# Router logits inside the normalisation, router parameters on SyncE's queue, and one stage for collecting the experts' rows and the final norm

## The reference

```python
def hier_moe(h, w_rg, b_rg, w_re, b_re, w_gate, w_up, w_down):
    ...
    g_logits = hf @ w_rg.astype(jnp.float32) + b_rg.astype(jnp.float32)
    ...
    top_v, top_i = lax.top_k(e_in_group, TOP_K)
    weights = jax.nn.softmax(top_v, axis=-1) * g_w
    ...
    def expert_block(args):
        xi, e = args
        return (jax.nn.silu(xi @ w_gate[e]) * (xi @ w_up[e])) @ w_down[e]
```

## Time and profile before

| | |
|---|---|
| median of three runs | 4025.27 us (4022.03 to 4025.39) |
| the profiled execution | 4030.13 us, its span 4028.2 us |
| TensorE busy | 3414.9 us, 85% of the span |
| VectorE, ScalarE, GpSimd busy | 39%, 27%, 16% |
| mean granted clock of TensorE | 0.922 |
| moved by DMA | 534.00 MB, mean 133 GB/s |

### The profile page before, as it was taken

The page is one execution under the profiler, slowest core; times in us unless marked ns, Lnnn a source line. Parts: engine busy times, 40 slices in busy tenths (PEclk is TensorE's granted clock), DMA queues, the critical chain, the costliest instruction groups (busy, mean ns, idle before and its releaser), DMA issues.

```text
span 4028.2 us, 41123 instructions
## 1 busy us (share of the span) xinstructions
PE 3414.9 (85%) x16083; PEld 2352.7 (58%) x16083; DVE 1570.6 (39%) x2654; ACT 1107.3 (27%) x1925; POOL 647.8 (16%) x471
## 2 busy tenths in 40 slices
PE   4996765787882998788999799999599888988998
PEld 2664543222231884445886488888485456856886
DVE  3226642000004356563333433333474563425444
ACT  3112411112112225443221222221234543303221
POOL 1000001000003325122220100000245223401000
PEclk8998876889996999899999899999799999998999
DMA  6883022799995311002112211111521002233222
GB/s 257 334 314 128 1 105 65 304 427 428 428 429 195 100 44 22 9 1 84 63 63 94 94 63 63 63 63 50 176 81 33 9 35 101 85 110 120 89 93 79
DMA packets 159784, 534.00 MB, mean 133 GB/s; under 512 B 9532, under 2 KB 64724, under 8 KB 136572
## 3 DMA queue, kind: packets, MB, share of 16 engines
q1 hardware_dynamic: 136252, 401.04, 26.9%
q0 software_dynamic: 16880, 92.26, 6.6%
q10 hardware_dynamic: 6480, 38.34, 2.4%
HBM read 488.84 MB, written 42.78 MB: 132 GB/s over the span
## 4 chain that ended last, share of the span: by engine, by line
PE 59%; DVE 4%; ACT 2%; DVEq 1%; DMA 1%; issue 1%; POOL 0%; ACTq 0%; POOLq 0%
PE ps L2774 11%; PE ps L2780 11%; PE ps L1840 7%; PE ps L1842 7%; PE ps L1841 7%; PE ps L511 5%; PE ps L2053 4%; PE ps L2105 2%; PE ps L2093 2%; PE ps L2087 1%; DVE Z L2677 1%; DMA ring<-in_w_out_dram 1%; DVE small L2193 0%; DVE hT_hi L2681 0%; DMA xl<-xspill 0%
## 5 line engine op out<-in xcount | busy, mean ns | idle before, releaser
L2774 PE MATMUL ps<-hT_hi,w_hi 128*128 128x512 f32 (+1 forms) x768 | 275.6, 359 | 27.9 <-DVE w_lo L2828 27.9
L2774 PE MATMUL ps<-hT_hi,w_lo 128*128 128x512 f32 (+1 forms) x768 | 276.4, 360 | 0.0
L2774 PE MATMUL ps<-hT_lo,w_hi 128*128 128x512 f32 (+1 forms) x768 | 275.8, 359 | 0.0
L1840 PE MATMUL ps<-wp_hi,hT_hi 128*128 128x512 f32 (+2 forms) x608 | 222.6, 366 | 37.2 <-POOL wp_lo L1819 37.2
L2780 PE MATMUL ps<-w_hi,h_hi 128*128 128x512 f32 x640 | 253.7, 396 | 0.0
L2780 PE MATMUL ps<-w_hi,h_lo 128*128 128x512 f32 x640 | 253.7, 396 | 0.0
L2780 PE MATMUL ps<-w_lo,h_hi 128*128 128x512 f32 x640 | 253.6, 396 | 0.0
L2053 PE MATMUL ps<-Z 64*128 64x256 f32 (+3 forms) x576 | 202.1, 548 | 28.2 <-DVE small L2195 12.5
L2493 POOL TENSOR_TENSOR mr_lo<-ring,wm_hi 128x2048 fp32r<-128x2048 f32 x36 | 170.7, 4754 | 312.1 <-ACT wm_hi L2485 312.0
L1842 PE MATMUL ps<-wp_hi,hm_lo 128*128 128x512 f32 (+2 forms) x608 | 220.8, 363 | 0.0
L1841 PE MATMUL ps<-wp_lo,hT_hi 128*128 128x512 f32 (+2 forms) x608 | 220.2, 362 | 0.0
(11 more groups left out here) (443 smaller groups left out, 6492.7 us busy)
## 6 DMA issues: line engine op xcount, KB each, us to landing
pj<-in_expert_w_up_dram SPq DMA_DIRECT2D x32, 2048.0 KB, 18.3
pj<-in_expert_w_down_dram SPq DMA_DIRECT2D x32, 2048.0 KB, 19.7
ring<-in_expert_w_gate_dram SPq DMA_DIRECT2D x32, 2048.0 KB, 15.9
ring<-in_ffn_w_dram SPq DMA_DIRECT2D x64, 1024.0 KB, 5.2
ring<-in_w_in_dram SPq DMA_DIRECT2D x58, 1024.0 KB, 5.3
Z<-in_w_mod_dram POOLq DMA_DIRECT2D x24, 2048.0 KB, 8.1
Z<-in_w_ada_dram POOLq DMA_DIRECT2D x8, 2048.0 KB, 9.0
ring<-in_w_out_dram SPq DMA_DIRECT2D x6, 2048.0 KB, 16.2
```

What stands on the lines that cost most here:

```text
L1840: nc.tensor.matmul(out_, a_hi, b_hi, start=first, stop=False)
L2774: last = nc.tensor.matmul(bank(i % 8, c1 - c0), W[a][:, k, :], r[:, k, c0:c1], start=(k == 0 and r is hhk and a == 0), stop=(k == KT - 1 a ...
```

## The change

- The logits of tile t are computed inside the normalisation, as soon as its evacuations are in, behind the transposes of tile t + 1. `pe_norm` calls `each` for this. They go to bank 4. The fence between normalisation and routing is gone.
- The seven parameter loads are issued by SP, one stage earlier, ahead of the context tile and the experts' first weights. Their place in `Z` moves.
- `fng` and the gates are loaded at the start of the experts' stage.
- The collection has buffers for all four tiles, in `pj`, so that the eight gathers are issued without a wait. ScalarE makes the first of the four passes over a tile (scaling by the first weight) and squares each tile when VectorE has added it. Collection and final norm are one stage.

```diff
                     last.then_inc(mm_done, 1)
+                if t:
+                    each(p, t - 1)
+            each(p, nt - 1)
             n["xn"] += nt
...
         XK = lambda t: Z[:, 1024 + 1024 * t:2048 + 1024 * t]
-        rw = Z[:, 5200:5488].rearrange("p (k n) -> p k n", k=KT)
-        rb = Z[:, 5488:5524]
+        rw = Z[:, 10240:10528].rearrange("p (k n) -> p k n", k=KT)
+        rb = Z[:, 10528:10564]
...
-        def pool_route_params(pool):
-            pool.dma_start(rw[:, :, 0:NG], I["router_group_w"][0].rearrange("(k p) n -> p k n", p=P)).then_inc(rparams, 16)
-            pool.dma_start(rw[:, :, NG:NG + NE], I["router_expert_w"][0].rearrange("(k p) n -> p k n", p=P)).then_inc(rparams, 16)
-            pool.dma_start(rb[:, 0:NG], I["router_group_b"][0].partition_broadcast(P)).then_inc(rparams, 16)
-            pool.dma_start(rb[:, NG:NG + NE], I["router_expert_b"][0].partition_broadcast(P)).then_inc(rparams, 16)
+        def sp_route_params(sp):
+            sp.dma_start(rw[:, :, 0:NG], I["router_group_w"][0].rearrange("(k p) n -> p k n", p=P)).then_inc(rparams, 16)
+            sp.dma_start(rw[:, :, NG:NG + NE], I["router_expert_w"][0].rearrange("(k p) n -> p k n", p=P)).then_inc(rparams, 16)
+            sp.dma_start(rb[:, 0:NG], I["router_group_b"][0].partition_broadcast(P)).then_inc(rparams, 16)
+            sp.dma_start(rb[:, NG:NG + NE], I["router_expert_b"][0].partition_broadcast(P)).then_inc(rparams, 16)
             for dst, src in ((fsh, modd[0, 0, 3 * D:4 * D]), (fsc, modd[0, 0, 4 * D:5 * D]), (fga, I["norm_ffn_g"][0])):
-                pool.dma_start(dst, src.rearrange("(p k) -> p k", k=KT)).then_inc(rparams, 16)
+                sp.dma_start(dst, src.rearrange("(p k) -> p k", k=KT)).then_inc(rparams, 16)
+
+        def pool_route_rows(pool):
             pool.memset(ZERO, 0).then_inc(zero_ok, 1)
...
+        def pe_logits(pe):
+
+            def each(p, t):
+                if t == 0:
+                    pe.wait_ge(rparams, 16 * 7)
+                for i in (2 * t, 2 * t + 1):
+                    pe.wait_ge(EV[p.own[i]], p.val[i])
+                for k in range(KT):
+                    last = nc.tensor.matmul(bank(4)[:, 36 * t:36 * t + 36], hTk[:, k, 128 * t:128 * t + 128], rw[:, k, :],
+                                            start=(k == 0), stop=(k == KT - 1))
+                if t == TL - 1:
+                    last.then_inc(mm_done, 1)
+            return each
+
         def pe_route(pe, n):
             p = plan_route(n)
-            pe.wait_ge(rparams, 16 * 7)
-            for t in range(TL):
-                for k in range(KT):
-                    last = nc.tensor.matmul(bank(0)[:, 36 * t:36 * t + 36], hTk[:, k, 128 * t:128 * t + 128], rw[:, k, :],
-                                            start=(k == 0), stop=(k == KT - 1))
-            last.then_inc(mm_done, 1)
             n["v2p"] += 1
...
                 for u in range(t + 1):
-                    last = nc.tensor.matmul(bank(1)[:, 32 * t:32 * t + 32], C(C_US) if u == t else C(C_ONE), oh[:, u, :],
+                    last = nc.tensor.matmul(bank(5)[:, 32 * t:32 * t + 32], C(C_US) if u == t else C(C_ONE), oh[:, u, :],
                                             start=(u == 0), stop=(u == t))
...
             for u in range(TL):
-                last = nc.tensor.matmul(bank(2)[:, 0:32], C(C_ONE), oh[:, u, :], start=(u == 0), stop=(u == TL - 1))
+                last = nc.tensor.matmul(bank(6)[:, 0:32], C(C_ONE), oh[:, u, :], start=(u == 0), stop=(u == TL - 1))
             last.then_inc(mm_done, 1)
...
-        yg = [[Z[:, 1024 * (2 * i + c):1024 * (2 * i + c) + 1024] for c in range(2)] for i in range(2)]
+        yg = [[pj[:, 1024 * (2 * i + c):1024 * (2 * i + c) + 1024] for c in range(2)] for i in range(TL)]
         fng = Z[:, 4608:5632]
...
-        def pool_comb(pool, n):
+        def pool_comb(pool):
             for t in range(TL):
-                if t >= 2:
-                    pool.wait_ge(yg_free, t - 1)
                 for c in range(2):
-                    pool.indirect_dma_start(yg[t % 2][c], None, ybuf, bass.IndirectOffsetOnAxis(ap=IDX[:, c, t:t + 1].bitcast(U32), axis=0)
-                                            ).then_inc(yg_in[t % 2], 16)
+                    pool.indirect_dma_start(yg[t][c], None, ybuf, bass.IndirectOffsetOnAxis(ap=IDX[:, c, t:t + 1].bitcast(U32), axis=0)
+                                            ).then_inc(yg_in[t], 16)
...
             for t in range(TL):
-                dve.wait_ge(yg_in[t % 2], 32 * (t // 2 + 1))
-                y0, y1 = yg[t % 2]
-                nc.vector.tensor_scalar(y0, y0, WT[0][:, t:t + 1], None, ALU.mult)
-                dve.drain()
+                dve.wait_ge(y0_ok, t + 1)
+                y0, y1 = yg[t]
                 nc.vector.scalar_tensor_tensor(y0, y1, WT[1][:, t:t + 1], y0, ALU.mult, ALU.add)
...
         def act_final(act, n):
-            act.wait_ge(yg_free, TL)
-            for t in range(TL):
-                act.activation(junk, xl[:, t, :], ACT.Square, accum_out=st[:, t:t + 1])
-                act.drain()
+            for t in range(TL + 1):
+                if t < TL:
+                    act.wait_ge(yg_in[t], 32)
+                    act.activation(yg[t][0], yg[t][0], ACT.Copy, scale=WT[0][:, t:t + 1]).then_inc(y0_ok, 1)
+                if t:
+                    act.wait_ge(yg_free, t)
+                    act.activation(junk, xl[:, t - 1, :], ACT.Square, accum_out=st[:, t - 1:t])
+                    act.drain()
             act.activation(st[:, 16:20], st[:, 0:4], ACT.Copy).then_inc(sumsq, 1)
...
             sp.wait_ge(stage_done, 4 * 10)
+            sp_route_params(sp)
             sp.dma_start(xl[:, TL:TA, :], I["ctx_2"][0].rearrange("(t p) d -> p t d", p=P)).then_inc(x_in, 16)
...
             plan_route(n)
-            sp.wait_ge(stage_done, 4 * 13)
+            sp.wait_ge(stage_done, 4 * 12)
             sp_moe(sp)
-            n["fence"] = 4 * 16
+            n["fence"] = 4 * 14
             plan_attn(n, *da_spec())
-            sp.wait_ge(stage_done, 4 * 16)
+            sp.wait_ge(stage_done, 4 * 14)
             for l in range(2):
...
                 fence(pool, n)
-            pool_route_params(pool)
-            fence(pool, n)
+            pool_route_rows(pool)
             pool_route(pool)
...
             fence(pool, n)
+            pool.dma_start(fng, I["final_norm_g"].partition_broadcast(P)).then_inc(fng_in, 16)
             pool_moe(pool)
             fence(pool, n)
-            pool.dma_start(fng, I["final_norm_g"].partition_broadcast(P)).then_inc(fng_in, 16)
-            pool_comb(pool, n)
-            fence(pool, n)
+            pool_comb(pool)
             fence(pool, n)
...
             fence(pe, n)
-            pe_norm(pe, n, TL, keep=XK)
-            fence(pe, n)
+            pe_norm(pe, n, TL, keep=XK, each=pe_logits(pe))
             pe_route(pe, n)
...
             pe_moe(pe)
-            fence(pe, n)
             fence(pe, n)
...
             act_norm(act, n, TL, 0, 1)
-            fence(act, n)
             act_route(act, n)
...
             fence(act, n)
+            load_gate(act, 0, 5)
             act_moe(act)
-            fence(act, n)
-            load_gate(act, 0, 5)
             fence(act, n)
...
             dve_norm(dve, n, TL, 0, 1, keep=XK)
-            fence(dve, n)
             dve_route(dve, n)
...
             dve_comb(dve, n)
-            fence(dve, n)
             dve.wait_ge(fng_in, 16)
...
             fence(dve, n)
```

More of the change, by code:

```diff
@@ L213, in program @@
         ex_used, ybz = sem("ex_used"), sem("ybz")
-        yg_in, fng_in = [sem("yg_in0"), sem("yg_in1")], sem("fng_in")
+        yg_in, fng_in, y0_ok = [sem(f"yg_in{i}") for i in range(4)], sem("fng_in"), sem("y0_ok")
         def tally():
```

10 lines of the change are left out of this document (5 added, 5 removed).

## The result

The changed kernel took 4002.87 us (median of 6 runs, 3997.96 to 4010.23), the kernel before 4027.38 beside it (median of 6). The ratio of the changed kernel's time to the time before is 0.9941, 95% interval 0.9926 to 0.9956: faster by 0.6%, some 24 us. The forecast was 3997.3 with a range of 3991 to 4007, so the time lies in the range, and the forecast gain of 28.0 was some 4 us too much.

The account below looks back on a forecast made before the run. Serial stretches before and after the experts' DMA-bound weight stream were taken to bound what can be saved. 17.4 - 1.5 + 12.1 = 28.0 us off the median 4025.27 gives 3997.3, range 3991 to 4007.

Parts of the forecast that it names:

- Logits: Normalisation: logits between transposes, no fence, bring VectorE's bias add 17.4 us earlier, bounds 14.3 and 20.4.
- the middle: Logits' end taken as 657.9, between 661.0 at 1.2 GHz and 654.9 at 2.4 GHz; gain 17.4 us.
- The upper bound: Logits at 2.4 GHz from 644.8, ending at 654.9: gain 20.4 us; part of a rival given 15 in 100.
- Parameters through SyncE: Seven small loads in SyncE's queue ahead of the weights: cost nothing, covered 68 us; weights out some 8 us later.
- The same 22 us of VectorE work follow: Routing behind the logits: VectorE's work unchanged, so GpSimd's first scatter moves along with the bias add.
- part 1: Logits computed within the normalisation, fence removed: gain 17.4 us.
- The moved loads: Start of the experts: fng by GpSimd, gates by ScalarE; cost 1.5 us, from 0 to 3.7.
- Contention: Start of the experts: moved loads share bandwidth with the first gather, at most 2.8 us within the 3.7 bound.
- Collection and final norm: Behind the experts: gathers without buffer waits, ScalarE scaling, one square left at the end; gain 12.1 us, bounds 9.3 and 12.7.
- Part 3: The change to collection and final norm: gain 12.1 us.
- The stream carried its start along: Experts' weight stream keeps its length, 508 to 509 us; second trip's SP loads about 16 us earlier. Opposite rival: 5 in 100.
- gathers as slow as before: Rival at the collection: 8.1 us landing is the gathers' own, gain there 9.3, sum 25.2, 4000.1 us; 17 in 100 for this end.

Follow-up runs that it names:

- e7: e5 plus 512-column filler matmuls on TensorE ahead of the normalisation, behind the logits, behind the rank matmuls and ahead of the experts' loop; 3992.65 us, ratio 0.9904.
- e9: e5 with all four tiles' transposes ahead of all logits, one stage, no fence, no fillers; 3998.67 us, ratio 0.9918.
- e11: e5 plus filler matmuls ahead of the normalisation, behind the logits and behind each of the first three logit groups; 3991.04 us, ratio 0.9905.
- e3: Kernel before with only the logits inside the normalisation and the parameters by SyncE; 4013.75 us, ratio 0.9967.
- e5: Changed kernel with fng and only the gate row that is read loaded by SyncE behind the first expert weights, into pj's unused end; 3995.62 us, ratio 0.9916.
- e10: Changed kernel with the seven parameter loads issued by GpSimd at the start of the normalisation again, without the fence; one run, 4013.83 us.
- e4: Kernel before with only the new collection, gates and fng loaded by ScalarE at the start of the experts; 4020.49 us, ratio 0.9982.
- e2: Changed kernel with the two gates loaded at the start of the collection again, fng still by GpSimd ahead of its loop; one run, 4002.57 us.
- e1: Changed kernel with fng issued by ScalarE behind the gates instead of by GpSimd ahead of its loop; 4004.86 us, ratio 0.9945.

## Why the prediction came out as it did

- **Logits: the mechanism right, the size off within its bounds.** Forecast 17.4 as the middle of 14.3 and 20.4; the profile gave 14.7, which is the end at 1.2 GHz, with its unit price of 3.47 a tile exact (the earlier trace rows against 647.89, 3.47). Among the profiles of programs with this order and no fillers the middle does not occur: they fall at 20.6 or at 13.0 us, to the bias add. The upper bound (20.4) was itself low, for 35.26 - 13.06 is 22.2; at the higher clock 32 records of logits took 3.66 us, 1.83 a tile, and not the 2.18 priced as transposes. Values between exist where the clock changed on the way under another program (e7 17.9, e9 and e11 16.0). Six profiles don't say how often each level comes, so the middle as a mean over executions is not shown either. The rule of the Trainium skill that the prediction weighed (TensorE: Matmul & The Clock Gate, part 1, the HAM clock gate), sustained matmul activity releases the throttle, holds in the profiles of e3 and e5 and not in those of the changed kernel and of before, where 20.5 and 13.87 us of unbroken work stayed at 0.50, nor at the end of e9's logits, where the clock fell during such work.
- **Parameters through SyncE: right at no cost, wrong in the numbers.** Seven loads were expected to take SP 8 us; they took 3.6 (574.66 to 578.22), the weights went out 2.8 us later than before (578.70 against 575.89), and each parameter landed 1.9 to 2.6 us after its issue. The prediction priced the change of queue at nothing beside the logits. e10 shows that it carried 9.7 us of them. It also called the zeroing the dearest per byte, 23.6 us for 12 KB; of the parameters in the same queue before, one of 2 KB took 9.9 us, which is dearer.
- **The routing chain: not foreseen, 1.6 gained.** "The same 22 us of VectorE work follow" did not hold to the end: 22.04 to the first scatter before, 20.13 now. ScalarE's table load for the exponential, 1.28 us, moved. Before it ran behind the bias add (as in e4's row), and VectorE waited 1.62 us for the exponential; with the fence gone it runs at 653.82, while ScalarE has nothing to do, and the wait is 0.28. All profiles with part 1 and without fillers show 31.8 for the chain, the two with the fence 33.4. The other 0.3 lie with GpSimd: its first scatter went out 0.53 us after the start of VectorE's last result and not 1.09, and from there to the read-back it took 11.68 and not 11.40.
- **The moved loads: the step that failed.** The prediction said 1.5 with a bound of 3.7, from the issue and contention. The profile gave 5.2: the copy came 0.4 later behind the read-back, for the issue, and the gap between copy and gather grew by 4.8. What it left out is the drain in GpSimd's loop, which does not only flush the copy but stands until GpSimd's own transfers have landed. Contention, on which the bound was built, cost the gather itself nothing in the changed kernel, since the drain held it back until the loads were over (4.7 us to the transposes, as before); it lengthened the load that the drain waits for, 6.1 us against 4.0 in e2. Where GpSimd has no load of its own (e1, e4) the gather took 2.1 and 1.7 us longer. And the evidence lay in the earlier trace rows: the prediction itself explains by the same behaviour, 637.45 + 23.6 = 661.05, why the fence opened when it did, and then it did not ask which other drain of GpSimd's had a transfer ahead of it.
- **Collection and final norm: right.** 12.0 against 12.1. The first pair took 6.6 us to ScalarE's pass, the number forecast (1233.1 - 1226.54), VectorE ran at 3.8 a tile without a wait, and from the last square to the next stage took 8.16 (8.15 in the earlier trace rows). Part 3 alone in e4 has the same 31.6.
- **The stream carried its start along: right.** SP's loads of the second trip went out at 721.96 instead of 734.93, 13.0 earlier and not the 16 expected. The first transposes came 12.0 earlier, which is the 16 less 2.7 for the clock and 3.7 for the drain, with 1.6 for the table load and 0.8 from ahead of the stretch added; the last 1.0 is in the first trip's gate matmuls (8.49 us, 9.51 before). From the trip's first gather to the collection's it took 508.4 us (509.5 before), inside the 508 to 509 of the forecast.
- **The sum.** 14.7 + 1.6 - 5.2 + 12.0 = 23.1, against 28.0 forecast and 23.8 by the ratio (0.0059 of 4027). The missing 4.9 is -2.7 for the clock, -3.7 for the drain and +1.6 for the table load. Parts 1 and 3 by themselves gave 0.33% and 0.18%, together 0.51% with an uncertainty of 0.16% against 0.59%, so no interaction of theirs can be told. No rival came true; the size is nearest to that of "gathers as slow as before", but for a reason that it did not have. The time lies in the range because the range had been drawn wide for that rival, and in that part it is luck. So is the agreement of the two profiled executions, 28.6 apart against 28.0: 5.4 of it stands in the ledger's first, fifth and last lines, which the sum does not have.

## What to carry to other kernels

When a load is moved to an engine's queue, look not only at what is queued behind it but at every drain that this engine meets before the load has landed, since each of them may become a wait for the transfer. Give loads with time to spare to a queue whose engine has no drain in its loop (here SyncE, some 110 us ahead of the experts: worth 5 us there), and check the same clue everywhere once a profile has shown it in one place. Where a stretch hangs on the clock that is granted, take bounds from both levels, and say that an execution may run at either all through or change between them on the way (e7), so that a middle is a guess about many executions and not a forecast of one.

## What the runs showed of the hardware

- GpSimd's drain returns 0.8 to 0.9 us after the landing of its own outstanding load, in three kernels with landings at 702.4, 704.3 and 705.7, and in e10 (715.7 and 716.53). A gather behind such a load without a drain between goes out at once (1227.42, 0.31 us idle).
- The same seven parameter loads land 1.9 to 2.6 us after issue in SyncE's queue, and 8.0 to 16.7 us in GpSimd's (e10). Queue and neighbours differ in these two; which of them matters was not separated.
- 20.5 us of TensorE work without a pause left the clock at 0.50 in four profiles, and in two others, whose normalisation is the same code, it rose in the window 643 to 644. It also fell during work without a pause, in e7 (643 to 644, 0.86) and e9 (652 to 653, 0.74). What decides that is open.
- ScalarE's table load for the exponential runs behind the bias add where a fence stands ahead of the routing (677.22 before, 677.60 in e4) and ahead of it where none does (653.82): 1.3 us of the chain.
